# Two loops of weight products in runs of eight, and three tensors moved by 64 bytes

## The chip, the core and the metric

The kernel runs on one core of one Trainium2 chip. The metric is the device time of the whole program in microseconds (us), as the median of several runs. All data are float32 in memory; the large products use the float32r form of TensorE's operands.

## The reference

The reference runs a token sequence of 256 positions, 2048 features wide, through two transformer-like blocks. Nearly all its arithmetic is projections, `x @ W`, with 256 rows on the left:

```python
h = x
for layer in range(DEPTH):                       # DEPTH = 2
    hn = rmsnorm(h, norm_w[layer])
    if layer % 2 == 0:
        h = h + hybrid_layer(hn, ...)            # h @ w_in (gated delta rule + dilated attention), @ w_out
    else:
        h = h + shortconv_layer(hn, ...)         # h @ w_in, causal convolution, @ w_out
x = rmsnorm(h, final_norm_w)
...
h = rms_norm(x, norm_mix_g[l]) * (1.0 + sc1) + sh1
proj = h @ w_in[l]                               # u, q, k, v, two gates
y_ssm, y_att = s5_branch(u, ...), moba_attention(q, k, v, rel_bias)
merged = sigmoid(ga) * (y_ssm @ w_proj_ssm[l]) + sigmoid(gb) * (y_att @ w_proj_attn[l])
x = x + g1 * (merged @ w_out[l])
h2 = rms_norm(x, norm_mlp_g[l]) * (1.0 + sc2) + sh2
x = x + g2 * (square(relu(h2 @ w_ff1[l])) @ w_ff2[l])   # 2048 -> 8192 -> 2048
return rms_norm(x, norm_final_g[l])
```

## The kernel before

**Split products.** A float32 weight is split in two float32r parts, `wh` (the high half, a rounded copy of `raw`, written by ScalarE at line 976) and `wl` = `raw` - `wh` (the low half, written by VectorE at line 1520, by GpSimd at line 1449 for some slabs). The activations are split likewise: for each chunk k of 128 features `xs[:, k, :]` holds the high part of the 256 positions in its first 256 columns and the low part in the next 256. One product of `wh` with all 512 columns and one of `wl` with the first 256 give the three partial products that are kept. They are called the wide and the narrow product below. Every product has a weight load (LDWEIGHTS, PEld in the profile) of 128 columns, which TensorE does beside the product ahead of it.

**Slabs and groups.** The weights come from memory as a stream of 936 slabs of 128 partitions x 1024 values (4096 bytes a partition), through rings of RING = 4 slots in `raw`, `wh` and `wl`. A slab has SLAB_K = 2 chunks of the contraction (k) for SLAB_N = 4 chunks of output (n). A group is the whole contraction for four output chunks: 8 slabs for the 104 groups of 2048 features, 4 slabs for 14 groups, 12 slabs for 4 groups. Each output chunk n has a PSUM bank `G[n]` ("gemm" in the profile); wide products write all 512 columns of it, narrow ones add to columns 256 to 511.

**The order on TensorE.** The function `group` (L521 on) writes it out. For each slab it waits for `hi_ready` and `lo_ready`, then for n = 0..3 it issues two wide products (k = 0, 1; L537) and two narrow ones (L542). I call these four one quad; a slab is four quads, 16 products. The last narrow product of the slab raises `slab_used`, on which ScalarE, VectorE and GpSimd wait before they overwrite that slot. In a group's first slab (sl = 0) each n first waits for its PSUM bank to be free, and in the last slab the last product of each n raises `bank_ready`. After n = 1 and after n = 3 a hook is called (slots 2*sl and 2*sl+1). It puts other, small products ("side" in the profile) between the quads: the steps of the delta rule and of attention, which go back and forth between TensorE, VectorE and ScalarE. In the heads' loop, for example, L670 (slot 10, 16, ...), VectorE L1735, L677 (the next slot), VectorE L1741 and the transposes of L682 follow each other. VectorE and ScalarE walk the same slots (`walk`), and at the start of each slab they first split the slab three ahead.

**The moving operands.** They are `xs` (the norm's output: 640 slabs) and `hid` or `hid2`, two names for one place (the kept activations of the layers' inner results: 296 slabs).

**Places in SBUF.** `place` puts tensors one behind the other from byte 16512 of each partition, rounded up to 32 bytes: `raw` 16512, `wh` 32896, `wl` 49280, `xs` 65664, then `tmp`, `vec`, `cst`, `mod`, `norm_g`, `parts`, `nrm`, `rn`, `mhalf`, `dnh`, and `hid` 108096. Chunks of `xs` and `hid` are 2048 bytes apart, the 128-column pieces of `wh` and `wl` 512 bytes, so that all of a tensor's pieces have one remainder modulo 512. Counted from `wh`, that remainder is 0 for `wl` and `xs` and 448 (64 bytes below a multiple) for `hid`. One more tensor, `wab2` (the weights of 16 products of 512 columns in a row at L606, with `xs` moving), is 16384 bytes behind `hid` and so has `hid`'s remainder.

Of the kernel before, what the change touches and what calls it, by code (L numbers as in the profile page):

```python
# [18 lines left out]
P = 128  # L19
T = 256  # L20
D = 2048
KC = D // P
# [20 lines left out]
SLAB_K = 2  # L43
SLAB_N = 4
# [53 lines left out]
def wait(eng, sem, value):  # L98

    if isinstance(value, int) and value <= 0:  # L100
        return
    eng.wait_ge(sem, value)


def program(nc, stack, ins, out_d):

    base0 = 16512
    top = [base0]
    named = [0]

    def place(name, shape, dt=F32):
        n = 4
        for s in shape[1:]:
            n *= s
        n = (n + 31) // 32 * 32
        t = nc.alloc_sbuf_tensor_at(name, list(shape), dt, offset=top[0])
        top[0] += n
        assert top[0] <= 229368, (name, top[0])
        return t

    raw = place("raw", [P, RING, SLAB])
    wh = place("wh", [P, RING, SLAB], F32R)
    wl = place("wl", [P, RING, SLAB], F32R)
    xs_at = top[0]
    xs = place("xs", [P, KC, 2 * T], F32R)
    tmp = place("tmp", [P, 4, T])
    vec = place("vec", [P, VEC_N])
    cst = place("cst", [P, CST_N])
    mod = place("mod", [P, 96])
    norm_g = place("norm_g", [P, KC])  # L130
    parts = place("parts", [P, 2 * 96])
    nrm = place("nrm", [P, 8])
    rn = place("rn", [P, 8])
    mhalf = place("mhalf", [P, 8])
    dnh = place("dnh", [P, 8])
    hid_at = top[0]
    hid = place("hid", [P, 24, 2 * T], F32R)
    arena = top[0]
    hid2 = nc.alloc_sbuf_tensor_at("hid2", [P, 32, 2 * T], F32R, offset=hid_at)
# [170 lines left out]
    def sem(name):  # L310
        return stack.enter_context(nc.semaphore(name))

    G = [stack.enter_context(nc.psum_tensor(f"gemm{n}", [P, 512], F32)) for n in range(4)]
# [12 lines left out]
    slab_used = sem("slab_used")  # L326
# [24 lines left out]
    def wait_lo(eng, q, slot):  # L351

        wait(eng, lo_ready[slot], q + 1)
# [168 lines left out]
    def _(pe):  # L522
        mm = nc.tensor.matmul

        def group(g, q0, nslabs, rhs, ready, hook=None, slot0=0):

            for sl in range(nslabs):
                q, slot = q0 + sl // RING, sl % RING
                wait(pe, hi_ready, 4 * q + slot + 1)
                wait_lo(pe, q, slot)  # L530
                ready(sl)
                for n in range(SLAB_N):
                    if sl == 0:
                        wait(pe, bank_freed, 4 * g + n - 3)
                    for k in range(SLAB_K):
                        at = (k * SLAB_N + n) * P
                        mm(G[n][:, :], wh[:, slot, at:at + P], rhs(sl * SLAB_K + k), start=sl == 0 and k == 0,  # L537
                           stop=False, skip_group_check=True)
                    for k in range(SLAB_K):
                        at = (k * SLAB_N + n) * P  # L540
                        last = sl == nslabs - 1 and k == SLAB_K - 1
                        op = mm(G[n][:, T:2 * T], wl[:, slot, at:at + P], rhs(sl * SLAB_K + k)[:, 0:T], start=False,  # L542
                                stop=last, skip_group_check=True)
                    if n == SLAB_N - 1:
                        op.then_inc(slab_used, 1)
                    elif sl == nslabs - 1:
                        op.then_inc(bank_ready, 1)
                    if hook is not None and n % 2 == 1:
                        hook(slot0 + 2 * sl + n // 2)
# [213 lines left out]
        for gi in range(3):  # L763
            group(gi, 2 * gi, 8, xs_of, xs_wait(0), lambda slot: gates(GATE_PE.get(slot)), 16 * gi)
        pe.wait_ge(loads["hyb"], 32)

        with pe.Fori(1, QK_HEADS) as h:
            for gi in range(3):
                group(3 * h + gi, 6 * h + 2 * gi, 8, xs_of, lambda sl: None, heads(h - 1), 16 * gi)
# [8 lines left out]
        for gi in range(3):  # L778
            group(G_OUTA + gi, Q_OUTA + 2 * gi, 8, hid_of(outa_chunks), outa_ready, heads(7), 16 * gi)
# [129 lines left out]
        for n, (q, count) in enumerate(ATT_GROUPS):  # L909
            rhs = (xs_of if n in ATT_GATES else (lambda k: hid2[:, 16 + k, :]) if n in ATT_GLU else  # L910
                   (lambda k: hid2[:, k, :]))
            ready = (lambda sl: None) if n in ATT_GATES else glu_ready if n in ATT_GLU else ssm_in
# [1561 lines left out]
```

## Time and profile before

| | |
|---|---|
| median of 3 runs | 3021.74 us (3021.52 to 3024.36) |
| the profiled execution's own time | 3025.32 us |
| its span, first to last instruction | 3023.3 us |
| mean granted TensorE clock | 0.990 of 2.4 GHz |
| wide / narrow products | 7488 / 7488 |

The profile is of one execution. A row of its timeline has the start in us, the duration in us, engine, line, operation and operands, and xN where N equal instructions that follow each other were merged; the duration then runs from the first one's start to the last one's end. A single matmul's duration includes its way through the array, so that two neighbours overlap: the pace is read from start to start, never from durations.

### The profile page before, as it was taken

What the parts mean: (1) busy time and instruction counts of PE and PEld (TensorE: products, weight loads), DVE (VectorE), ACT (ScalarE), POOL (GpSimd) and SP (SyncE); (2) the same over time, 40 slices, a digit from 0 to 9 for tenths busy, and PEclk for the clock granted to TensorE, in tenths of its full rate; (3) what the DMA queues carried; (4) which work ended last, traced back from release to release, by engine and by line L of the source; (5) the groups of instructions that cost most, each with busy time, mean ns of one, the idle gap of its engine ahead of it and who ended that gap; (6) DMA issues with size and microseconds to landing.
All of it is one profiled execution on the core that took longest, in us unless ns stands there. A gap on an engine that the chain in (4) does not pass through costs nothing.

```text
span 3023.3 us, 51503 instructions
## 1 busy us (share of the span) xinstructions
PE 2953.2 (98%) x17546; PEld 2572.6 (85%) x17546; DVE 2152.5 (71%) x3020; ACT 1506.3 (50%) x2164; POOL 452.1 (15%) x187
## 2 busy tenths in 40 slices
PE   7999999999999999999998999999999999999998
PEld 6889898889987888888887877788887888888887
DVE  6666666676568888888877899876687426565465
ACT  4454444544444444444444777766544444444443
POOL 0111011110100000000000000000002445545443
PEclk9999999999999999999998999999999999999999
DMA  6444434444457887888885545456785566766655
GB/s 214 143 138 132 136 131 142 139 139 146 147 192 254 311 298 282 317 303 303 301 294 172 166 168 168 166 194 211 246 303 172 188 210 223 243 236 236 206 182 174
DMA packets 172690, 629.41 MB, mean 208 GB/s; under 512 B 19224, under 2 KB 20376, under 8 KB 171808
## 3 DMA queue, kind: packets, MB, share of 16 engines
q1 hardware_dynamic: 165024, 601.99, 57.6%
q10 hardware_dynamic: 7552, 25.91, 2.5%
q8 instruction: 71, 1.16, 0.2%
q14 instruction: 43, 0.35, 0.0%
HBM read 615.22 MB, written 12.60 MB: 208 GB/s over the span
## 4 chain that ended last, share of the span: by engine, by line
PE 69%; issue 24%; DVE 4%; ACT 2%; DMA 1%; DVEq 0%; POOL 0%; SPq 0%; ACTq 0%; POOLq 0%
PE gemm L537 42%; PE gemm L542 21%; PE side L670 1%; PE side L677 1%; DVE wl L1520 1%; ACT wh L976 1%; PE side L682 1%; PE side L563 0%; DMA raw<-in_stream 0%; DMA x<-in_x 0%; PE side L737 0%; DVE gB L1711 0%; ACT gA L1078 0%; DVE xs L1599 0%; PE side L714 0%
## 5 line engine op out<-in xcount | busy, mean ns | idle before, releaser
L537 PE MATMUL gemm<-xs,wh 128*128 128x512 f32 x5120 | 1649.6, 404 | 28.7 <-DVE xs L1599 8.6
L976 ACT ACTIVATE wh<-raw 128x1024 fp32r<-128x1024 f32 x939 | 984.4, 1058 | 925.9 <-PE gemm L542 799.6
L1520 DVE TENSOR_TENSOR wl<-raw,wh 128x1024 fp32r<-128x1024 f32 x811 | 1035.7, 1281 | 451.2 <-ACT wh L976 428.7
L542 PEld LDWEIGHTS gemm<-xs,wl 128*128 128x128 f32 x5120 | 967.1, 189 | 229.4
L542 PE MATMUL gemm<-xs,wl 128*128 128x256 f32 x5120 | 1013.2, 279 | 0.0
L537 PEld LDWEIGHTS gemm<-xs,wh 128*128 128x128 f32 x5120 | 786.4, 190 | 56.5 <-issue 50.8
L537 PE MATMUL gemm<-hid,wh 128*128 128x512 f32 x2368 | 748.5, 397 | 6.7 <-DVE fxg L1525 2.2
L542 PEld LDWEIGHTS gemm<-hid,wl 128*128 128x128 f32 x2368 | 446.8, 189 | 102.0
L542 PE MATMUL gemm<-hid,wl 128*128 128x256 f32 x2368 | 468.8, 279 | 0.0
L1449 POOL TENSOR_TENSOR wl<-raw,wh 128x1024 fp32r<-128x1024 f32 x128 | 348.8, 2730 | 370.5 <-ACT wh L976 370.5
L537 PEld LDWEIGHTS gemm<-hid,wh 128*128 128x128 f32 x2368 | 358.4, 189 | 9.7 <-ACT wh L976 3.3
L1455 POOL TENSOR_TENSOR rn<-nrm,mhalf 128x2 f32<-128x2 f32 (+1 forms) x5 | 3.8, 762 | 1473.8 <-DVE nrm L1576 779.3
L986 ACT ACTIVATE tmp<-gemm 128x256 f32<-128x256 f32 x408 | 152.7, 381 | 81.1 <-PE gemm L542 71.4
L1842 DVE SCALAR_TENSOR_TENSOR ada_a<-ada_a,cond 128x1024 f32<-128x1024 f32 x144 | 175.5, 1219 | 0.0
L1525 DVE TENSOR_TENSOR fx<-gemm,tmp 128x256 f32<-128x256 f32 x96 | 38.4, 421 | 81.3 <-ACT tmp L986 79.0
L1475 POOL TENSOR_TENSOR rn<-nrm,mhalf 128x4 f32<-128x4 f32 x8 | 13.9, 1743 | 530.1 <-DVE nrm L1752 530.1
L1093 ACT ACTIVATE Em<-side 128x512 f32<-128x512 f32 x48 | 28.8, 600 | 106.8 <-PE side L682 106.8
L1842 DVE SCALAR_TENSOR_TENSOR ada_b<-ada_b,cond 128x1024 f32<-128x1024 f32 x48 | 76.1, 1585 | 0.0
L1741 DVE TENSOR_TENSOR Dm<-side,Dm 128x256 f32<-128x256 f32 x48 | 20.3, 424 | 45.3 <-PE side L677 45.3
L670 PE MATMUL side<-Dm,AT 128*128 128x64 f32 x384 | 48.8, 270 | 1.8 <-DVE Em L1728 1.7
L670 PEld LDWEIGHTS side<-Dm,AT 128*128 128x128 f32 x384 | 46.7, 191 | 3.4 <-DVE Em L1728 3.4
L677 PE MATMUL side<-Xm,Em 128*128 128x64 f32 x384 | 48.1, 268 | 0.0
(377 smaller groups left out, 1951.4 us busy)
## 6 DMA issues: line engine op xcount, KB each, us to landing
raw<-in_stream SPq DMA_DIRECT2D x940, 512.0 KB, 3.8
ada_a<-in_ada SPq DMA_DIRECT2D x144, 512.0 KB, 5.0
ada_b<-in_ada SPq DMA_DIRECT2D x48, 512.0 KB, 5.1
stash<-stage ACTq DMA_DIRECT2D x12, 512.0 KB, 3.0
att<-stash ACTq DMA_DIRECT2D x8, 384.0 KB, 4.0
x<-in_x SPq DMA_DIRECT2D x4, 512.0 KB, 5.7
xacc<-in_x ACTq DMA_DIRECT2D x1, 2048.0 KB, 11.2
stash<-stA ACTq DMA_DIRECT2D x4, 512.0 KB, 6.5
```

What stands on the lines that cost most here:

```text
L537: mm(G[n][:, :], wh[:, slot, at:at + P], rhs(sl * SLAB_K + k), start=sl == 0 and k == 0, stop=False, skip_group_check=True)
L542: op = mm(G[n][:, T:2 * T], wl[:, slot, at:at + P], rhs(sl * SLAB_K + k)[:, 0:T], start=False, stop=last, skip_group_check=True)
L670: op = mm(ps0[:, j * 64:(j + 1) * 64], AT[:, j, :], left, start=True, stop=True)
L677: op = mm(ps0[:, 256 + j * 64:256 + (j + 1) * 64], Em[:, j, :], Xm[:, j, :], start=True, stop=True)
L682: op = nc.tensor.transpose(ps1[:, j * P:(j + 1) * P], Dm[:, j, :], ident)
L976: A(wh[:, slot, :], raw[:, slot, :], ACT.Copy).then_inc(hi_ready, 1)
L986: A(tmp[:, n, :], G[n][:, T:2 * T], ACT.Copy).then_inc(tmp_ready, 1)
L1093: A(Em[:, :, :], ps1[:, :], ACT.Copy).then_inc(S("a_E"), 1)
L1449: nc.gpsimd.tensor_tensor(wl[:, slot, :], raw[:, slot, :], wh[:, slot, :].bitcast(F32), ALU.subtract).then_inc(lo_ready[slot], 1)
L1520: tt(wl[:, slot, :], raw[:, slot, :], wh[:, slot, :].bitcast(F32), ALU.subtract).then_inc(lo_ready[slot], 1)
L1525: tt(out, G[n][:, 0:T], tmp[:, n, :], ALU.add).then_inc(bank_freed, 1)
L1842: stt(s_, s_, 0.5, cond[:, half * SLAB:half * SLAB + SLAB], ALU.mult, ALU.mult, accum_out=parts[:, bass.ds(t0 + m, 1)]).then_inc(S("ada_us ...
```

## The change

Three things are done.

1. In `group`, every slab but a group's first and last (0 < sl < nslabs-1: 692 of the 936 slabs, 480 with `xs` moving and 212 with `hid`) runs its eight wide products first and then its eight narrow ones. It waits for `hi_ready` before the wide ones and for `lo_ready` only ahead of the narrow ones. The first hook of such a slab stands between the eight and the eight, the second behind all 16.
2. `nrm` and `rn` (32 bytes each) stand between `wh` and `wl`, so that `wl` lies 64 bytes past a multiple of 512 counted from `wh`; `mod` and `norm_g` (448 bytes) follow `wl`, so that `xs` keeps the remainder 0.
3. 64 bytes of padding ahead of `hid` bring its remainder from 448 to 0. All that lies behind it moves by 64 bytes, `wab2` too.

No product, wait or transfer is added or dropped. The diff:

```diff
     raw = place("raw", [P, RING, SLAB])
+    wh_at = top[0]
     wh = place("wh", [P, RING, SLAB], F32R)
+    nrm = place("nrm", [P, 8])
+    rn = place("rn", [P, 8])
+    wl_at = top[0]
     wl = place("wl", [P, RING, SLAB], F32R)
+    mod = place("mod", [P, 96])
+    norm_g = place("norm_g", [P, KC])
     xs_at = top[0]
...
-    mod = place("mod", [P, 96])
-    norm_g = place("norm_g", [P, KC])
     parts = place("parts", [P, 2 * 96])
-    nrm = place("nrm", [P, 8])
-    rn = place("rn", [P, 8])
     mhalf = place("mhalf", [P, 8])
     dnh = place("dnh", [P, 8])
+    top[0] += (wh_at - top[0]) % 512
     hid_at = top[0]
+    assert (xs_at - wh_at) % 512 == 0 and (hid_at - wh_at) % 512 == 0 and (wl_at - wh_at) % 512 == 64
     hid = place("hid", [P, 24, 2 * T], F32R)
...
         def group(g, q0, nslabs, rhs, ready, hook=None, slot0=0):
 
+            def high(sl, slot, n, k):
+                at = (k * SLAB_N + n) * P
+                mm(G[n][:, :], wh[:, slot, at:at + P], rhs(sl * SLAB_K + k), start=sl == 0 and k == 0, stop=False,
+                   skip_group_check=True)
+
+            def low(sl, slot, n, k):
+                at = (k * SLAB_N + n) * P
+                return mm(G[n][:, T:2 * T], wl[:, slot, at:at + P], rhs(sl * SLAB_K + k)[:, 0:T], start=False,
+                          stop=sl == nslabs - 1 and k == SLAB_K - 1, skip_group_check=True)
+
             for sl in range(nslabs):
                 q, slot = q0 + sl // RING, sl % RING
                 wait(pe, hi_ready, 4 * q + slot + 1)
+                if 0 < sl < nslabs - 1:
+                    ready(sl)
+                    for n in range(SLAB_N):
+                        for k in range(SLAB_K):
+                            high(sl, slot, n, k)
+                    if hook is not None:
+                        hook(slot0 + 2 * sl)
+                    wait_lo(pe, q, slot)
+                    for n in range(SLAB_N):
+                        for k in range(SLAB_K):
+                            op = low(sl, slot, n, k)
+                    op.then_inc(slab_used, 1)
+                    if hook is not None:
+                        hook(slot0 + 2 * sl + 1)
+                    continue
                 wait_lo(pe, q, slot)
                 ready(sl)
                 for n in range(SLAB_N):
                     if sl == 0:
                         wait(pe, bank_freed, 4 * g + n - 3)
                     for k in range(SLAB_K):
-                        at = (k * SLAB_N + n) * P
-                        mm(G[n][:, :], wh[:, slot, at:at + P], rhs(sl * SLAB_K + k), start=sl == 0 and k == 0,
-                           stop=False, skip_group_check=True)
+                        high(sl, slot, n, k)
                     for k in range(SLAB_K):
-                        at = (k * SLAB_N + n) * P
-                        last = sl == nslabs - 1 and k == SLAB_K - 1
-                        op = mm(G[n][:, T:2 * T], wl[:, slot, at:at + P], rhs(sl * SLAB_K + k)[:, 0:T], start=False,
-                                stop=last, skip_group_check=True)
+                        op = low(sl, slot, n, k)
```

On TensorE in the heads' loop, two steps of the delta rule in one slab stood so before (L537 wide, L542 narrow, L670 and L677 side products, L102 the bookkeeping of a wait):

```order
L537 MATMUL gemm<-xs,wh 128x512 x2
L542 MATMUL gemm<-xs,wl 128x256 x2
L537 MATMUL gemm<-xs,wh 128x512 x2
L542 MATMUL gemm<-xs,wl 128x256 x2
L102 ISA
L670 MATMUL side<-Dm,AT 128x64 x4
L537 MATMUL gemm<-xs,wh 128x512 x2
L542 MATMUL gemm<-xs,wl 128x256 x2
L537 MATMUL gemm<-xs,wh 128x512 x2
L542 MATMUL gemm<-xs,wl 128x256 x2
L102 ISA
L677 MATMUL side<-Xm,Em 128x64 x4
```

The same slab on TensorE in the changed kernel, where the wide products are at L533, the narrow ones at L538 and the two side steps at L694 and L701:

```order
L533 MATMUL gemm<-xs,wh 128x512 x8
L102 ISA
L694 MATMUL side<-Dm,AT 128x64 x4
L538 MATMUL gemm<-xs,wl 128x256 x8
L102 ISA
L701 MATMUL side<-Xm,Em 128x64 x4
```

The first side step has moved from the middle of the slab's 16 products to behind the eight wide ones, which are two thirds of its columns; the second has kept its place at the slab's end.

## Rows read from the trace of the kernel before

**Rows 1.** The page's first part: busy us (share of the span), number of instructions.

```profile
PE 2953.2 (98%) x17546; PEld 2572.6 (85%) x17546; DVE 2152.5 (71%) x3020; ACT 1506.3 (50%) x2164; POOL 452.1 (15%) x187
```

**Rows 2.** The page's fourth part, the chain that ended last: shares by line.

```profile
PE gemm L537 42%; PE gemm L542 21%; PE side L670 1%; PE side L677 1%; DVE wl L1520 1%; ACT wh L976 1%; PE side L682 1%; PE side L563 0%; DMA raw<-in_stream 0%; DMA x<-in_x 0%; PE side L737 0%; DVE gB L1711 0%; ACT gA L1078 0%; DVE xs L1599 0%; PE side L714 0%
```

**Rows 3.** Waits of all engines and of TensorE: total us, times, longest us.

```profile
ACT wh L976 <- PE gemm L542: 799.6, 506, 5.4
DVE wl L1520 <- ACT wh L976: 428.7, 326, 4.3
PE side L563 <- DVE sq L1622: 13.1, 1, 13.1
PE gemm L537 <- DVE xs L1599: 8.6, 6, 3.1
PE gemm L537 <- DVE wl L1520: 0.6, 1, 0.6
```

**Rows 4.** Timeline, TensorE, where three stages of 32 slabs begin.

```profile
2651.52 0.39 PE L537 MATMUL gemm<-xs,wh 128*128 128x512 f32 x1
2740.71 0.40 PE L537 MATMUL gemm<-hid,wh 128*128 128x512 f32 x1
2829.46 0.39 PE L537 MATMUL gemm<-xs,wh 128*128 128x512 f32 x1
```

**Rows 5.** Timeline, TensorE, half clock: windows row (us, busy, PEclk), then starts.

```profile
915.00:924.00 9.00, 6.27 (x20) 0.50 0.43 155
...
919.48 1.05 PE L537 MATMUL gemm<-xs,wh 128*128 128x512 f32 x2
920.33 0.63 PE L542 MATMUL gemm<-xs,wl 128*128 128x256 f32 x2
920.76 1.05 PE L537 MATMUL gemm<-xs,wh 128*128 128x512 f32 x2
```

**Rows 6.** Timeline, TensorE, full clock, `xs` moving: two quads.

```profile
1008.24 0.63 PE L537 MATMUL gemm<-xs,wh 128*128 128x512 f32 x2
1008.71 0.39 PE L542 MATMUL gemm<-xs,wl 128*128 128x256 f32 x2
1008.94 0.62 PE L537 MATMUL gemm<-xs,wh 128*128 128x512 f32 x2
1009.40 0.40 PE L542 MATMUL gemm<-xs,wl 128*128 128x256 f32 x2
1009.64 0.63 PE L537 MATMUL gemm<-xs,wh 128*128 128x512 f32 x2
```

**Rows 7.** Timeline, TensorE: 16 products of 512 columns in a row.

```profile
59.18 3.84 PE L606 MATMUL side<-xs,wab 128*128 128x512 f32 x16
```

**Rows 8.** Line L606 alone: duration in ns min/median/max.

```profile
L606 PE MATMUL side<-xs,wab x16: 388/392/397, 59.2 to 62.6; 128*128 128x512 f32 x16
```

**Rows 9.** Timeline, weight loads (PEld) of two narrow, then two wide products.

```profile
1000.82 0.42 PEld L542 LDWEIGHTS gemm<-xs,wl 128*128 128x128 f32 x2
1001.16 0.31 PEld L537 LDWEIGHTS gemm<-xs,wh 128*128 128x128 f32 x2
1001.51 0.42 PEld L542 LDWEIGHTS gemm<-xs,wl 128*128 128x128 f32 x2
```

**Rows 10.** Timeline, heads' loop, one slab with two side steps, all engines.

```profile
231.50 0.72 PE L537 MATMUL gemm<-xs,wh 128*128 128x512 f32 x2
...
233.00 1.00 PE L670 MATMUL side<-Dm,AT 128*128 128x64 f32 x8
233.44 1.23 DVE L1520 TENSOR_TENSOR wl<-raw,wh 128x1024 fp32r<-128x1024 f32 x1 [2.09 <-ACT wh L976]
...
234.59 0.42 DVE L1735 TENSOR_TENSOR Xm<-side,hyc 128x256 f32<-128x256 f32 x1
...
235.28 1.00 PE L677 MATMUL side<-Xm,Em 128*128 128x64 f32 x8
```

## The prediction

> **What bounds the kernel now.** I read the busy shares first, then the chain, the waits, and last the timeline of TensorE from start to start. TensorE is busy for 98% of the span, the other engines for 71% at most [rows 1]. The chain that ended last has 42% in the wide products of L537 and 21% in the narrow ones of L542 [rows 2]; much of the rest of it is issue time between the same instructions. The producers wait for TensorE and not it for them: ScalarE stands 799.6 us before its splits until the gemm of L542 is done with a slot, while the gemm waited once, for 0.6 us, for a low half [rows 3]. So the end is set by the pace of 3744 quads, plus the side products between them, and what any other engine does is covered as long as TensorE doesn't come to wait.
>
> **The pace, and what is too much in it.** A stage of 32 slabs is 128 quads. With `xs` moving it took 2740.71 - 2651.52 = 89.19 us, or 0.697 us a quad; with `hid` moving 2829.46 - 2740.71 = 88.75 us, or 0.693 us [rows 4]. A quad streams 2 x 512 + 2 x 256 = 1536 columns, 0.640 us at 2.4 GHz. At half clock nothing is added to the columns: 920.76 - 919.48 = 1.28 us a quad, which is 1536 columns at 1.2 GHz to the last digit [rows 5]. So at full clock each quad has a surplus of 0.057 us (`xs`) or 0.053 us (`hid`), about 0.014 and 0.013 for each product. Over all 640 x 4 and 296 x 4 quads that is 146 + 63 = 209 us: this is all that the change can work on. Within a quad the pair of wide products takes 0.46 to 0.47 us and the pair of narrow ones 0.23 to 0.24 [rows 6], so both kinds carry some of the surplus (0.427 and 0.213 would be the columns).
>
> The two moving tensors have the same shapes, order and weights. They differ in where they lie: `xs` at remainder 0 to both halves, `hid` 64 bytes below. The 0.004 us a quad between them is the only sign in the trace that places matter.
>
> **The change part by part.**
>
> *Runs of eight.* No product goes away. A middle slab takes 4 x 0.697 = 2.787 us now with `xs`, 4 x 0.693 = 2.773 with `hid`. The trace of before has one uninterrupted run of wide products, 16 of them: from the first start to the last end 3.84 us [rows 7], less the 0.392 of one product [rows 8], is 3.45 us for 15 steps, 0.230 us each. Its weights lie 64 bytes below the moving operand's remainder, which is neither the relation before nor the one after, but it is the only run, so I take it: 8 x 0.230 = 1.840 us. For narrow products there is no run longer than two. Half of the pair's 0.23 us is 0.115 [rows 6]; the ends are 0.107 (256 columns alone) and 0.120 (below, the loads' pace). I take 0.115, which is nearest to what stands in the rows: 8 x 0.115 = 0.920. A middle slab is then 2.760 us. That is 0.027 less for 480 slabs with `xs`, 13.0 us, and 0.013 less for 212 slabs with `hid`, 2.8 us. Together **-16 us**.
>
> The same run argues against a bigger gain from the order alone. It has no switch between wide and narrow, and yet a surplus of 0.230 - 0.213 = 0.017 us on each product, no less than the quads' average of 0.014. So the surplus isn't a price of the switches, of which a slab has eight now and two afterwards (that reading would have saved three quarters of it).
>
> *The remainders.* After the change both moving tensors lie at 0 to `wh` and 64 bytes below `wl`. Each relation is in the trace of before, but mixed: `xs` has 0 with both halves, `hid` 64 below with both. If each product kept the surplus of its relation, an `xs` slab would gain (0.057 - 0.053) x 4 / 2 = 0.007 us and a `hid` slab would lose as much: 640 slabs less 296, -2.4 us, which is near nothing. For the 244 slabs that keep the old order I take zero, between -0.007 and +0.007 us a slab. What a run makes of these relations no row shows; that is the main unknown, and both ends are below.
>
> *The first hook of a slab* stands behind 8 wide products instead of behind two quads: 1.84 us into the slab instead of 1.39, so 0.45 later, and the time to the next hook shrinks from 1.39 to 0.92. Where a side step answers one at the hook before, the work between them on VectorE has 0.45 us less. The tightest such place: L670 at 233.00, VectorE's Xm at 234.59 to 235.01, L677 at 235.28, 0.27 us later [rows 10]. But Xm didn't start on L670's end (234.00): VectorE was in the split of a slab, from 233.44 to 234.67. With L670 ending at 234.45 the split still ends last, and L677 keeps its 0.27 us. I cost it at zero; the cover is that split, and without it L677 would wait 0.18 us, 24 times in all (8 heads, three such steps of six in each), 4 us.
>
> *The later wait for `lo_ready`* can save the 0.6 us that was waited once [rows 3]. Behind it stand only the slab's narrow products, and the low half was awaited earlier before. ScalarE and VectorE get the slot back with the same last product as before. Zero. The moved `nrm`, `rn`, `mod` and `norm_g` are small operands of the same engines: zero.
>
> Sum: 3025.3 - 16 = 3009 us in the profiled execution's terms. Its time is 3.6 us above the median of the runs, so the forecast for the median is 3021.7 - 16 = **3006 us**.
>
> **The rivals.**
>
> *The relations free the reads (gain much larger).* If the surplus is the moving stream and the weight load meeting in SBUF, a run of equal products holds one relation from product to product, and a good one could avoid most meetings. Before, no product had equal neighbours on both sides. For it: the surplus is absent at half clock [rows 5], as it is when the two streams need less in the same time, and the two places of the moving tensor differ by 0.004 us a quad. Against it: the run of rows 7 holds one relation and has the full surplus. If half of the middle slabs' surplus goes, it is (0.227 x 480 + 0.213 x 212) / 2 = 77 us: 2945 us. If a quarter goes, 2983.
>
> *No change.* The relations' surplus is kept as it was, product by product (-2.4 us, above), and runs are worth nothing: 3019 to 3022 us. The Trainium skill speaks for this one, and against the change: "TensorE: Matmul & The Clock Gate", Part 2, has two independent read ports, one for the moving operand and one for the weights, so that loading the next weights takes nothing from the running product; by that rule neither places nor runs matter and the time is 3021.7 us. The surplus at full clock and the 0.44 us between the stages of rows 4 are not explained by it, but at 0.4 us in 89 they bear little against it either.
>
> *Slower: narrow runs at the loads' pace.* A weight load is 128 columns whatever it is for. Above a wide product it has 0.23 us, above a narrow one only 0.115. The two loads ahead of wide products start 0.12 us apart (0.31 less 0.19) and those of narrow ones 0.23 (0.42 less 0.19) [rows 9]: a load that is late over one narrow product is made up for in the next wide one. In a run of eight nothing makes up for it. With 0.120 for each narrow and 0.230 for each wide product the slab is 2.800 us: +0.013 x 480 + 0.027 x 212 = +12 us, 3034. With 0.233 for the wide ones, what `xs` has now on average, it is 2.824: +0.037 x 480 + 0.051 x 212 = +29, 3050. It decides from where a narrow product in a run takes more than (2.787 - 1.840) / 8 = 0.118 us. Against it: the narrow pairs of now are at 0.115 to 0.12 each without loss to the wide pairs.
>
> **How the numbers follow.** Forecast (2998 to 3014 us): 0.38. Relations free the reads (2945 to 2990): 0.20. No change: 0.20. Slower: 0.22. About 0.2% (6 us) is what a measurement of this kernel can tell from no change, so faster is 0.38 + 0.20 = 0.58, same 0.20, slower 0.22. The range takes in half of the middle slabs' surplus gone at the low end, 2947, and the slower case's first value with some of its second, 3040. The likeliest case is in the faster part; its own range is 2998 to 3014.
>
> **What would show it.** The stage of 32 slabs with `xs` moving (89.19 us now) should take 89.19 - 24 x 0.027 = 88.5 us, the one with `hid` 88.75 - 24 x 0.013 = 88.4, so both nearly alike, since both now have the same relations. In the timeline a middle slab should show eight wide products starting 0.230 us apart and eight narrow ones 0.115. The freed reads would show as wide starts under 0.225 or narrow ones at 0.110; the slower case as narrow ones at 0.120 or more with the wide ones unchanged. L677 should still start 0.27 us or so behind the end of Xm, and the waits of TensorE for VectorE should not grow by more than 2 us in all. The forecast is wrong if wide products in a run depend on the relation far more than 0.001 us a product, which is all that the quads show of it now.

## The result and the profile after

The changed kernel takes 3036.6 us (median of 7 runs, 3033.4 to 3044.0) against 3023.3 us before (7 runs): a ratio of 1.0047, with an interval of 1.0036 to 1.0058. It is slower by 0.5%. The forecast was 3006 us, faster than before; the measured time lies within its range (2947 to 3040 us), but on the slower side. The medians are 13 us apart, the profiled executions (3025.3 and 3033.5 us) only 8; the profiled one of the changed kernel is among its shortest, and their mean granted clock goes from 0.991 in the shortest to 0.988 in the longest.

The page of the changed kernel, its first part and its clock row (wide products now at L533, narrow at L538, ScalarE's split at L1000, VectorE's at L1544, the two side steps at L694 and L701):

```profile
span 3031.5 us, 51186 instructions
...
PE 2955.5 (97%) x17546; PEld 2573.8 (85%) x17546; DVE 2159.8 (71%) x3020; ACT 1506.2 (50%) x2164; POOL 445.9 (15%) x187
...
PEclk9999999999999999999998999999999999999999
```

Shares (but for 1% of TensorE's) and counts are those of [rows 1], and the span has grown by 8.2 us. Where, the timeline of TensorE tells. First the end of the heads' stage, which is the first stage with `xs` moving, in the kernel before:

```profile
748.17 0.40 PE L537 MATMUL gemm<-hid,wh 128*128 128x512 f32 x1
```

and in the changed kernel:

```profile
760.08 0.40 PE L533 MATMUL gemm<-hid,wh 128*128 128x512 f32 x1
...
2659.50 0.40 PE L533 MATMUL gemm<-xs,wh 128*128 128x512 f32 x1
...
2748.62 0.40 PE L533 MATMUL gemm<-hid,wh 128*128 128x512 f32 x1
...
2837.74 0.40 PE L533 MATMUL gemm<-xs,wh 128*128 128x512 f32 x1
```

The heads' stage lasts 11.9 us longer; both stages begin at 18.4 us. Everything behind it together is 3.7 us shorter. The last three rows answer to [rows 4]: 89.12 us for 32 slabs with `xs` (89.19 before) and 89.12 with `hid` (88.75 before).

So the pace itself came out nearly even. Timeline of the changed kernel, TensorE, two middle slabs:

```profile
1006.75 2.00 PE L533 MATMUL gemm<-xs,wh 128*128 128x512 f32 x8
1008.59 1.11 PE L538 MATMUL gemm<-xs,wl 128*128 128x256 f32 x8
1009.53 2.00 PE L533 MATMUL gemm<-xs,wh 128*128 128x512 f32 x8
1011.37 0.87 PE L538 MATMUL gemm<-xs,wl 128*128 128x256 f32 x6
```

Eight wide products take 1.84 us, 0.230 each, as forecast. Eight narrow ones take 0.94 us, 0.1175 each, where 0.115 was forecast. A middle slab is 2.78 us.

The loss is in the side steps. Waits of TensorE, the kernel before and then the changed one (total us, times, longest us):

```profile
PE side L670 <- DVE Em L1728: 1.7, 6, 0.3
```

```profile
PE side L694 <- DVE Em L1752: 8.1, 6, 1.4
```

TensorE now stands up to 1.4 us before the delta rule's first level (VectorE writes its operand, Em). This is what makes VectorE late. Timeline of one head (the first) in the kernel before, GpSimd and VectorE; the bracket holds the engine's idle time before the instruction and what ended it:

```profile
109.32 1.23 DVE L1520 TENSOR_TENSOR wl<-raw,wh 128x1024 fp32r<-128x1024 f32 x1 [2.65 <-ACT wh L976]
109.48 3.32 POOL L1472 TENSOR_TENSOR bb<-bb,rb 32x1024 f32<-32x1024 f32 x1
110.47 1.12 DVE L1711 SCALAR_TENSOR_TENSOR gB<-side,beta,gB 128x128 f32<-128x128 f32 x4
...
112.10 1.00 DVE L1718 TENSOR_TENSOR qe<-qkv,eg 128x256 f32<-128x256 f32 x1
...
117.94 0.68 DVE L1728 TENSOR_TENSOR Em<-Em,cst 128x512 f32<-128x512 f32 x1
```

and the same head in the changed kernel:

```profile
109.50 2.38 POOL L1496 TENSOR_TENSOR bb<-bb,rb 32x1024 f32<-32x1024 f32 x1
109.66 3.31 DVE L1544 TENSOR_TENSOR wl<-raw,wh 128x1024 fp32r<-128x1024 f32 x1 [2.65 <-PE gemm L538]
...
112.89 1.11 DVE L1735 SCALAR_TENSOR_TENSOR gB<-side,beta,gB 128x128 f32<-128x128 f32 x4
...
114.53 0.41 DVE L1742 TENSOR_TENSOR qe<-qkv,eg 128x256 f32<-128x256 f32 x1
...
119.78 0.68 DVE L1752 TENSOR_TENSOR Em<-Em,cst 128x512 f32<-128x512 f32 x1
```

Before, VectorE's split started 0.16 us ahead of GpSimd's addition; the split took 1.23 us and the addition 3.32. Now the addition starts 0.16 us ahead; it takes 2.38 us and the split 3.31. VectorE's next operations are 2.4 us late. Em, for which TensorE waits, is 1.8 us late, since qe takes 0.41 us now instead of 1.00. TensorE comes to its step 0.5 us later itself and waits for the rest.

The split itself is late by only 0.34 us. It waits on ScalarE's split, which stands in ScalarE's order behind the exponentials of the delta rule; these use VectorE's gB (L1702, now L1726, 0.33 us later), and that goes back to the side step of slot 2, a first hook of a slab, 0.47 us later now. Side step and ScalarE's split, before:

```profile
103.95 0.60 PE L637 MATMUL side<-cst,gsel 128*128 128x128 f32 x4
...
108.16 1.05 ACT L976 ACTIVATE wh<-raw 128x1024 fp32r<-128x1024 f32 x1
```

and in the changed kernel:

```profile
104.42 0.60 PE L661 MATMUL side<-cst,gsel 128*128 128x128 f32 x4
...
108.49 1.05 ACT L1000 ACTIVATE wh<-raw 128x1024 fp32r<-128x1024 f32 x1
```

ScalarE's split ends 0.11 us ahead of VectorE's before and 0.12 us ahead of it now, so I take it for what VectorE waited for in both, although the bracket of the later row names a product.

The other heads bear this out. Before, the split started first in each of them, by 0.12 to 0.27 us. In the changed kernel the addition is first in six heads, by 0.02 to 0.28 us, and these are the six in which TensorE waits, 1.35 us each time. In the third and the eighth head the split kept ahead, by 0.02 and 0.21 us, and TensorE doesn't wait there.

The Trainium skill states such a lock: "SBUF — State Buffer", section "Who interferes with whom", has a VectorE instruction with two SBUF inputs and a GpSimd one that reads SBUF exclude each other, the second waiting until the first is done. The trace agrees: the addition ends at 111.88, and 1.23 us from there would be 113.11, where the split ends at 112.97.

A second price comes on top. Windows of the changed kernel, TensorE (us, busy, PEclk), then of the kernel before:

```profile
121.00:125.00 4.00, 4.00 (x23) 0.58 0.65 240
217.00:221.00 4.00, 4.00 (x20) 0.57 0.54 188
688.00:692.00 4.00, 4.00 (x19) 0.57 0.45 157
```

```profile
121.00:125.00 4.00, 4.00 (x29) 1.00 0.42 139
217.00:221.00 4.00, 4.00 (x27) 1.00 0.39 131
688.00:692.00 4.00, 4.00 (x29) 1.00 0.47 146
```

After three of the six waits the clock fell to its lower level for 3.4 us, which costs half of that, 1.7 us each. The waits' 6.4 us more and 3 x 1.7 = 5.1 us for the clock are 11.5 of the 11.9 us by which the stage is longer.

### The profile page after: what moved, and what is told of

Its sections match the earlier page's. It is cut to its first block, busy times and chain, and to the rows that moved or that the text cites. A ratio compares the mean times of both kernels' runs of the same rounds, so it can differ in the third digit from the quotient of the medians.

```text
span 3031.5 us, 51186 instructions
## 1 busy us (share of the span) xinstructions
PE 2955.5 (97%) x17546; PEld 2573.8 (85%) x17546; DVE 2159.8 (71%) x3020; ACT 1506.2 (50%) x2164; POOL 445.9 (15%) x187
## 4 chain that ended last, share of the span: by engine, by line
PE 64%; issue 25%; DVE 6%; ACT 2%; DMA 2%; SPq 0%; DVEq 0%; POOL 0%; ACTq 0%; POOLq 0%
PE gemm L533 38%; PE gemm L538 19%; DVE wl L1544 2%; DMA raw<-in_stream 2%; PE side L701 1%; PE side L694 1%; ACT wh L1000 1%; PE side L706 1%; PE side L587 0%; DVE ada_a L1866 0%; DVE cc L1549 0%; DVE cc L1953 0%; DVE yv L1954 0%; DMA x<-in_x 0%; PE side L761 0%
## 5 line engine op out<-in xcount | busy, mean ns | idle before, releaser
L1000 ACT ACTIVATE wh<-raw 128x1024 fp32r<-128x1024 f32 x939 | 985.1, 1058 | 917.9 <-PE gemm L538 802.2
L533 PE MATMUL gemm<-xs,wh 128*128 128x512 f32 x5120 | 1394.1, 399 | 28.0 <-DVE xs L1623 8.4
L1544 DVE TENSOR_TENSOR wl<-raw,wh 128x1024 fp32r<-128x1024 f32 x811 | 1047.9, 1296 | 445.2 <-ACT wh L1000 402.9
L533 PEld LDWEIGHTS gemm<-xs,wh 128*128 128x128 f32 x5120 | 887.5, 189 | 169.9 <-issue 37.9
L538 PEld LDWEIGHTS gemm<-xs,wl 128*128 128x128 f32 x5120 | 758.7, 190 | 96.8 <-issue 9.8
L538 PE MATMUL gemm<-xs,wl 128*128 128x256 f32 x5120 | 802.2, 284 | 0.0
L533 PE MATMUL gemm<-hid,wh 128*128 128x512 f32 x2368 | 641.7, 396 | 7.5 <-DVE x L1576 2.3
L533 PEld LDWEIGHTS gemm<-hid,wh 128*128 128x128 f32 x2368 | 406.0, 188 | 64.7 <-issue 3.2
L538 PEld LDWEIGHTS gemm<-hid,wl 128*128 128x128 f32 x2368 | 355.9, 189 | 45.4
L538 PE MATMUL gemm<-hid,wl 128*128 128x256 f32 x2368 | 369.8, 281 | 0.0
L694 PEld LDWEIGHTS side<-Dm,AT 128*128 128x128 f32 x384 | 47.8, 191 | 12.9 <-DVE Em L1752 11.4
L694 PE MATMUL side<-Dm,AT 128*128 128x64 f32 x384 | 48.8, 270 | 8.1 <-DVE Em L1752 8.1
L701 PEld LDWEIGHTS side<-Xm,Em 128*128 128x128 f32 x384 | 50.4, 200 | 1.7
```

The source lines that it names most:

```text
L538: return mm(G[n][:, T:2 * T], wl[:, slot, at:at + P], rhs(sl * SLAB_K + k)[:, 0:T], start=False, stop=sl == nslabs - 1 and k == SLAB_K - 1 ...
L694: op = mm(ps0[:, j * 64:(j + 1) * 64], AT[:, j, :], left, start=True, stop=True)
L701: op = mm(ps0[:, 256 + j * 64:256 + (j + 1) * 64], Em[:, j, :], Xm[:, j, :], start=True, stop=True)
L1000: A(wh[:, slot, :], raw[:, slot, :], ACT.Copy).then_inc(hi_ready, 1)
L1544: tt(wl[:, slot, :], raw[:, slot, :], wh[:, slot, :].bitcast(F32), ALU.subtract).then_inc(lo_ready[slot], 1)
```

## Experiments

The theory: the later first hook swaps split and addition and so makes the heads' stage slow, while runs and places only move the pace by tenths of a per cent. The rivals: the new places cost the time; the runs are slow by themselves; the 0.47 us are what TensorE waits for, with no swap needed.

### The order alone

```diff
 # changed kernel
-    (the places of the change)
+    (the places of before: wl and xs at remainder 0, hid at 448, counted from wh)
```

> The change's order (eight wide, eight narrow, hooks behind them) with all tensors in their places of before. Theory (the later first hook makes the heads' loop wait, places matter little): the heads' stage (from the first product to the first with hid moving) stays near the changed kernel's 742 us, against 730 before; whole kernel 3030 to 3045 us; TensorE again waits over 6 us for VectorE's Em. Rival (the new places cost the time): heads' stage back to 730, whole kernel 3015 to 3024 us.

Measured: 3032.4 us (ratio 1.0034, 1.0021 to 1.0046), heads' stage 741.1 us, 8.0 us of waits for Em. The new places don't cause the loss in the heads. The 32-slab stages were 89.33 us (`xs`, against 89.19) and 88.76 (`hid`, 88.75): in the old places the runs are worth nothing, or slightly less.

### The places alone

> The new places with the order of before. Theory: heads' stage within 2 us of the 730 us of before; a 32-slab stage takes 89.2 to 89.7 us with xs and with hid moving alike (both have one set of relations now, quads near 0.700 us as in the first and last slabs of the changed kernel); whole kernel 3021 to 3032 us. Rival (the places cost the time in the heads' loop): heads' stage 740 us, whole kernel 3034 us or more.

Measured: 3038.0 us (ratio 1.0051, 1.0034 to 1.0067), heads' stage 731.0 us. The heads' stage and the pace are as the theory had them; the whole kernel, at most 3032 us by it, is a miss. Timeline, TensorE, two stages:

```profile
2661.98 0.40 PE L541 MATMUL gemm<-xs,wh 128*128 128x512 f32 x1
...
2751.58 0.40 PE L541 MATMUL gemm<-hid,wh 128*128 128x512 f32 x1
...
2841.18 0.40 PE L541 MATMUL gemm<-xs,wh 128*128 128x512 f32 x1
```

89.60 us each: 2.800 us a slab in the old order. That is 0.013 more for 640 slabs and 0.027 more for 296, 16 us, which is the whole loss of this kernel (15 us, against 3022.9 us for the kernel before in the same series). So the change's places cost 15 us by themselves, outside the heads' stage for the most part.

### The first hook back in its old time

```diff
                     for n in range(SLAB_N):
+                        if n == SLAB_N - 1 and hook is not None:
+                            hook(slot0 + 2 * sl)
                         for k in range(SLAB_K):
                             high(sl, slot, n, k)
-                    if hook is not None:
-                        hook(slot0 + 2 * sl)
```

> The changed kernel, with the first hook of a middle slab behind six wide products (6 x 0.23 = 1.38 us into the slab, as before) instead of eight. Theory: heads' stage back to 728 to 731 us, TensorE's wait for Em back under 2 us, VectorE's split in slab 2 of a head again starts before GpSimd's add; the other stages as in the changed kernel; whole kernel 3017 to 3022 us. Rival (the runs or the places are slow in the heads' loop for another reason): 3030 us or more, heads' stage still near 742.

Measured: 3022.1 us (ratio 0.9999, 0.9989 to 1.0009), heads' stage 728.3 us, waits for Em 2.1 us. Timeline of the same head as above, VectorE and GpSimd:

```profile
109.16 1.22 DVE L1544 TENSOR_TENSOR wl<-raw,wh 128x1024 fp32r<-128x1024 f32 x1 [2.65 <-ACT wh L1000]
```

```profile
109.31 3.34 POOL L1496 TENSOR_TENSOR bb<-bb,rb 32x1024 f32<-32x1024 f32 x1
```

With the hook behind six products the split is first again, in all eight heads, and the loss is gone. This gives the three parts of the change, from the medians: the places cost 15 us, the runs give 16 us of it back (3038.0 to 3022.1), and the later hook costs 14 (3022.1 to 3036.6; the kernel before took 3022.9 and 3023.3 us in the two series). In the heads' stage the later hook costs 13.4 us, 741.6 against 728.3.

### The later hook alone

```diff
 # kernel before
                     for k in range(SLAB_K): (wide products)
+                    later = 0 < sl < nslabs - 1
+                    if hook is not None and later and n == 2:
+                        hook(slot0 + 2 * sl)
                     for k in range(SLAB_K): (narrow products)
...
-                    if hook is not None and n % 2 == 1:
+                    if hook is not None and (n == 3 if later else n % 2 == 1):
```

> The kernel before, its order and places, with only the first hook of middle slabs moved from behind the second quad to behind the wide pair of the third, 0.47 us later. Theory: this alone brings the loss: heads' stage 738 to 745 us, TensorE waits over 6 us for Em, whole kernel 3030 to 3040 us. Rival (the hook's place is harmless, as the prediction had it): 3021 to 3024 us, heads' stage 730.

Measured: 3036.4 us (ratio 1.0045, 1.0028 to 1.0062), waits for Em 9.3 us, the split at 109.66 took 3.29 us, and the heads' stage 745.8 us (forecast up to 745), with three stretches of half clock in it. The addition was first in seven heads, and TensorE waited in these seven. The later hook alone brings the loss; pace and places are those of before.

### Without the addition on GpSimd

> The changed kernel without the third GpSimd instruction of the rotary step in the heads' loop (the addition of rb to bb, 2.4 us alone, 3.3 us in the kernel before); this leaves the sum out of the rotated q and k, so attention is computed from unrotated parts. Theory (in the changed kernel this addition starts just ahead of VectorE's split in slab 2 of a head, which then takes 3.2 us instead of 1.2 and makes all behind it late): the split in that slab takes 1.2 us again, TensorE's wait for Em falls from 8.1 us to under 2, no half clock in the heads' loop, heads' stage 727 to 731 us, whole kernel 3018 to 3024 us. Rival (the 0.45 us that the hook is later are themselves what TensorE waits for): the wait for Em stays over 5 us and the heads' stage over 737 us.

This kernel leaves out the addition, so that attention is computed from unrotated parts.

```diff
                     nc.gpsimd.tensor_tensor(rb[:, :, :], rb[:, :, :], sinb, ALU.mult)
-                    nc.gpsimd.tensor_tensor(qk, qk, cosb, ALU.mult).then_inc(S("b_cos"), 1)
-                    pool.wait_ge(S("b_cos"), it + 1)
-                    nc.gpsimd.tensor_tensor(qk, qk, rb[:, :, :], ALU.add).then_inc(S("b_rope"), 1)
+                    nc.gpsimd.tensor_tensor(qk, qk, cosb, ALU.mult).then_inc(S("b_rope"), 1)
```

Measured: 3015.0 us (ratio 0.9973, 0.9963 to 0.9983; eight of nine executions within 3013.1 to 3017.5 us, one of 5895 us), heads' stage 724.5 us, no wait for Em in the list of waits, no half clock in the heads. Timeline of VectorE:

```profile
109.70 1.23 DVE L1542 TENSOR_TENSOR wl<-raw,wh 128x1024 fp32r<-128x1024 f32 x1 [2.65 <-PE gemm L538]
```

The hook is as late as in the changed kernel and the split starts as late (109.70), but takes 1.23 us, and TensorE doesn't wait. So without the addition the lateness costs nothing. With it in place the third and the eighth head of the changed kernel say the same: late hook, split still ahead, no wait. What costs is the addition when it comes first. The stage is even 3.8 us shorter than with the hook in its old time, so the addition cost something before as well (qe, L1718, took 1.00 us beside it in the kernel before, and 0.41 in the changed kernel, where it is alone).

### The addition behind the split

```diff
                     pool.wait_ge(S("b_cos"), it + 1)
+                    pool.wait_ge(S("d_A"), it + 1)
                     nc.gpsimd.tensor_tensor(qk, qk, rb[:, :, :], ALU.add).then_inc(S("b_rope"), 1)
```

> The changed kernel, hook behind eight, with GpSimd's addition waiting for VectorE's gB of the same head, so that it can't start ahead of VectorE's split; all is computed. Theory (the order of the two is what costs): the split takes 1.2 us, TensorE's wait for Em under 3 us, heads' stage 726 to 732 us, whole kernel 3018 to 3026 us; the addition now meets VectorE's later operations, which costs those up to 1 us. Rival (the addition costs the same wherever it runs): heads' stage 737 us or more.

Measured: 3032.4 us (ratio 1.0036, 1.0023 to 1.005), heads' stage 740.1 us: a miss. Timeline, VectorE:

```profile
109.78 1.22 DVE L1545 TENSOR_TENSOR wl<-raw,wh 128x1024 fp32r<-128x1024 f32 x1 [2.65 <-PE gemm L538]
...
112.56 2.31 DVE L1743 TENSOR_TENSOR qe<-qkv,eg 128x256 f32<-128x256 f32 x1
```

The split is short again, as expected, but the addition (now from 112.19) caught the next operation with two SBUF inputs, which took 2.31 us instead of 0.41, in all eight heads. When Em was done, VectorE was as late as in the changed kernel (120.39 us, against 120.46 there and 118.62 before), and TensorE waited 10.7 us in eight pieces, 9.4 us of it in the heads' stage. The stage's time is the rival's, but its reason, that the addition costs the same wherever it runs, doesn't hold: with the split ahead of it (hook in its old time) the same addition left the stage at 728.3 us. What matters isn't the pair of split and addition, but that the addition runs first against one of VectorE's two-input operations on this chain. It cost least where the split ran ahead of it.

### The pace by places, alone

> Only products, nothing of the kernel's work: for each of 8 places of the wide weights and 8 of the narrow ones (0 to 448 bytes past a multiple of 512 counted from the moving operand, in steps of 64) four slabs in the order of before, then the same 64 pairs in runs of eight, with no other engine at work. Theory (each weight load costs the stream about 0.013 to 0.017 us whatever the places, and these move it by 1% at most): every slab between 2.76 and 2.83 us, runs and quads alike. Rival (a good relation frees the reads in a run): some pair at 2.70 us or less in runs of eight, and not in quads.

Its span was 1465.7 us, in one execution. The places repeat after 256 bytes: the values for 256 to 448 are those for 0 to 192 within 0.008 us, except for the first cell (in part at half clock), for which the table has the value 256 bytes on. The table has the us per slab, from the first product's start of one pair to that of the next, over four slabs; w and n are the places of wide and narrow weights behind the moving operand, modulo 256.

| | n 0 | n 64 | n 128 | n 192 |
|---|---|---|---|---|
| quads, w 0 | 2.786 | 2.801 | 2.800 | 2.775 |
| quads, w 64 | 2.848 | 2.777 | 2.799 | 2.774 |
| quads, w 128 | 2.824 | 2.826 | 2.789 | 2.818 |
| quads, w 192 | 2.793 | 2.774 | 2.799 | 2.764 |
| runs, w 0 | 2.793 | 2.781 | 2.806 | 2.787 |
| runs, w 64 | 2.809 | 2.784 | 2.812 | 2.802 |
| runs, w 128 | 2.804 | 2.780 | 2.810 | 2.794 |
| runs, w 192 | 2.786 | 2.749 | 2.799 | 2.768 |

The kernels are in it: `xs` before is quads (0, 0), 2.786 here and 2.787 there; `hid` before is quads (64, 64), 2.777 and 2.773; the places alone are quads (0, 64), 2.801 and 2.800; the changed kernel is runs (0, 64), 2.781 and 2.780. The order alone with `hid` moving fits least well, runs (64, 64): 2.784 here (2.776 at the place 256 bytes on) and 2.775 there. So the pace in the kernel is, to 0.01 us a slab, that of the products among themselves, with nothing from other engines. Neither side was quite right: no pair came to 2.70, but the quads span 2.764 to 2.848 and the runs 2.749 to 2.812, which is more than the 1% and the 2.76 to 2.83 that I gave. The best pair's rows, runs with wide weights at 448 ("wh" is that tensor's name here) and narrow ones at 64 ("nb"):

```profile
1380.25 2.01 PE L79 MATMUL gemm<-mov,wh 128*128 128x512 f32 x8
1382.10 1.07 PE L85 MATMUL gemm<-mov,nb 128*128 128x256 f32 x8
1383.01 2.00 PE L79 MATMUL gemm<-mov,wh 128*128 128x512 f32 x8
1384.84 1.07 PE L85 MATMUL gemm<-mov,nb 128*128 128x256 f32 x8
1385.76 2.00 PE L79 MATMUL gemm<-mov,wh 128*128 128x512 f32 x8
```

### `xs` in `hid`'s relation

> The kernel before with mod and norm_g ahead of xs, so that xs too lies 64 bytes below a multiple of 512 counted from both halves, as hid does; order and hooks as before. Theory: the stages with xs moving take on hid's pace, 88.75 us for 32 slabs instead of 89.19; 640 slabs x 0.014 us = 9 us less, 3012 to 3016 us. Rival (the pace hangs on the tensor or its stage, not on the place): xs stages stay at 89.2 us, 3021 to 3025 us.

Measured: 3018.8 us (ratio 0.9986, 0.9977 to 0.9995). The `xs` stages went to 88.75 us, like `hid`: the pace hangs on the place. The total fell by 4 us, not 9, which is neither the theory's 3012 to 3016 nor the rival's 3021 or more: the stages without side steps behind 2290 us took all of their share, the heads' stage only 1.1 of its 2.7 us and the second long stage (192 slabs as well) 0.6 of 2.7. Why, these runs don't tell.

### The best places, with runs and with quads

> The order of the changed kernel with the first hook behind six wide products, and the places that the run of products alone found best for runs: wide weights 64 bytes below, narrow weights 64 above a multiple of 256 counted from the moving operand (2.749 us a slab in runs, 2.774 in quads). Theory (the relations act in the kernel as in that run): the 32-slab stages take 24 x 2.75 + 8 x 2.774 = 88.2 us with either moving operand, heads' stage 720 to 725 us, whole kernel 2995 to 3004 us. Rival (ScalarE's, VectorE's and the transfers' accesses blur it): 88.7 us or more, whole kernel 3012 us or more.

The places against the changed kernel; the hook's edit is the one shown above:

```diff
     raw = place("raw", [P, RING, SLAB])
+    (nrm, rn, mhalf, dnh: 128 bytes)
     wh = place("wh", [P, RING, SLAB], F32R)
+    mod = place("mod", [P, 96])
     wl = place("wl", [P, RING, SLAB], F32R)
+    (norm_g, vec)
     xs = place("xs", [P, KC, 2 * T], F32R)
...
+    assert (xs_at - wh_at) % 256 == 64 and (hid_at - wh_at) % 256 == 64 and (wl_at - wh_at) % 256 == 128
```

Measured: 3006.4 us against 3022.0 (ratio 0.9952, 0.9938 to 0.9965). Timeline, TensorE:

```profile
2632.89 0.39 PE L532 MATMUL gemm<-xs,wh 128*128 128x512 f32 x1
...
2720.99 0.39 PE L532 MATMUL gemm<-hid,wh 128*128 128x512 f32 x1
...
2809.10 0.39 PE L532 MATMUL gemm<-xs,wh 128*128 128x512 f32 x1
```

88.10 and 88.11 us, where 88.2 was expected. The total missed its 2995 to 3004 by 2 us, again through the heads' stage: 727.7 us, no better than the 728.3 with the places of the change and the same hook, where 720 to 725 was expected.

> The kernel before, order and hooks unchanged, with the places that were best for quads: both halves 64 bytes below a multiple of 256 counted from the moving operand (2.764 us a slab). Theory: 32-slab stages 88.45 us, both alike, whole kernel 3003 to 3010 us. Rival: stages of 88.7 us or more, 3013 us or more.

Measured, for the order of before: 3010.2 us (ratio 0.9959, 0.9945 to 0.9973), stages 88.32 us both, heads' stage 727.5 us. Its median is 4 us above that of the runs, and the two intervals overlap.

### The hook earlier still

> As e8_best_relation, with the first hook behind four wide products (0.92 us into the slab). Theory (what counts in the heads' loop is which of VectorE's split and GpSimd's addition starts first): the split stays ahead, the stages outside the heads' loop as in e8, heads' stage within 3 us of e8's, either way. Rival (each shift of the hook costs by its size): heads' stage 5 us or more from e8's.

Measured: 3011.3 us (ratio 0.9962, 0.9947 to 0.9977), stages 88.11 us, heads' stage 730.6 us, 2.9 more than with the hook behind six. Here TensorE waited 5.8 us for Em, in 8 pieces of at most 0.8: it comes to the step of slot 10 earlier than VectorE, whose chain runs on its own time. That is a plain price of 0.46 us at a step without slack, not a swap. It is within the 3 us expected, just so.

## Why the prediction was wrong

Two terms that were put at nothing failed, and each is as large as the gain that was forecast: the later first hook cost 14 us, the new places 15. The first makes the kernel slower; without it (3022.1 us) the second would still have left nothing of the gain.

- **What bounds the kernel: right.** All totals above follow from the pace of TensorE and its waits. What the reading missed is that "covered as long as TensorE doesn't come to wait" already had no margin at one place: the kernel before waited for Em six times, 0.3 us at most. That row stands in the waits, and I passed over it.
- **The first hook: this is the step that turned the sign.** "I cost it at zero" went by one place, L670 to L677, and no wait shows there after the change either. The same 0.45 us were not followed through the other steps: slot 2's side step, VectorE's gB, ScalarE's exponentials and split, VectorE's split, GpSimd's addition. The prediction named no instruction on GpSimd at all. The price was 14 us in the medians and 13.4 us in the profiled heads' stages, shown by the hook alone (3036.4 us), by its return (3022.1), and by taking the addition away (no wait).
- **The remainders: the second step that failed.** "Near nothing" (-2.4 us) rested on each product keeping the surplus of its relation. In the old order the places cost 15 us instead (2.800 us a slab where the two unmixed relations had 2.787 and 2.773). The relations of wide and narrow weights don't add up one by one; each pair has a pace of its own.
- **Runs of eight: the sign held for `xs` alone, the size was off.** The term was 2.760 us a middle slab; it measured 2.780, which is 0.007 less than before with `xs` and 0.007 more with `hid`. The wide products were as forecast (0.230), the narrow ones 0.1175 instead of 0.115, 0.020 a slab, or 14 of the 16 us of gain. That the runs gave 16 us when added to the new places, the very number forecast, is luck: they brought 2.800 down to 2.780, not 2.787 to 2.760, and in the places of before they gave nothing in pace. Everything outside the heads gained 3.7 us, but the kernel with the later hook alone, at the pace of before, gained 3.9 us there, so that this isn't the runs' doing either.
- **The range.** The time lies in it, but its upper end stood for narrow products at the loads' pace, and that is not what happened: they stayed under that rival's limit of 0.118. The measured time is in the range for another reason than the one it was drawn for.
- **The rivals:** the slower one lost as a mechanism though its side won. The freed reads are refuted: the best slab, 2.749, keeps 0.189 of the 0.227 us of surplus, where that rival had a quarter to a half of it gone; in the kernel the best places were worth 16 us. "No change" had the time nearer than the forecast, but not its reason. The Trainium skill ("TensorE: Matmul & The Clock Gate", Part 2, two independent read ports) stood for it, with the reading that neither places nor runs matter. That reading fails here: with nothing but products running, places alone move a slab from 2.764 to 2.848 in quads and from 2.749 to 2.812 in runs. Whether it is the reads of weights and moving operand that meet, no run shows.

What stays open: why pairs of places differ as they do, why the kernel with the later hook alone was 3.9 us shorter outside the heads' stage (one profiled execution each), and why the heads' stage, in which side steps break up the runs, takes so little of a better pace (0.6 us of the 6 us that 192 slabs at 0.03 would give).

## What to carry to other kernels

When a step moves by half a microsecond, follow it to every queue that it reaches and look for two operations of VectorE and GpSimd that start within that time of each other: which of them is first was worth 2 us to VectorE each time here, and TensorE's wait behind it sometimes cost clock too. Check each edit of a bundle alone: here one cost 15 us, one gave 16 back and one cost 14. If operand places are in question, time the products alone at all places before arguing from two of them.

## What the runs showed of the hardware

- With float32r operands at full clock, the pace of products with their weight loads depends on where the weights lie to the moving operand modulo 256 bytes, and on the pair of places of two kinds of product that alternate: 2.764 to 2.848 us in quads and 2.749 to 2.812 in runs, for one and the same work of 6144 columns (2.560 us at 2.4 GHz). At half clock the columns alone set the pace [rows 5].
- A GpSimd operation on 32 partitions that started 0.16 us ahead of a VectorE one with two SBUF inputs made it 3.31 us long instead of 1.23; the other way round the GpSimd one grew from 2.38 to 3.32. A lead of 0.02 us was enough, either way.
- Waits of 1.3 to 1.4 us in TensorE's stream, between side steps, were followed by 3.4 us at the lower clock in three of six cases and left it up in the other three; in the kernel with the order alone, in one of six.
